# The squared tiles of a scan group summed on VectorE before the matmul with ones, and the sum moved one product on

## The chip, the cores and the metric

The kernel runs on one core of a Trainium2 chip. The metric is the device time of one execution in microseconds. TensorE does the matrix products into PSUM (eight banks of 128 partitions by 512 floats), VectorE and ScalarE do elementwise work, GpSimd a little of it, and SyncE starts the transfers. Each engine has its own program, in order; they are held together by semaphores.

## The reference

A trunk of two layers over 256 latent tokens and 256 context tokens of width 1024. Layer 0 has a mixer of Fourier channel groups and a bidirectional state-space scan (SSD) in four head groups of 384 channels; layer 1 has attention; each is followed by a squared-ReLU MLP. The change sits in the output of the scan:

```python
def ssd_output(y, xs, z, d_skip, norm_g):
    b, l = y.shape[:2]
    y = (y + d_skip[..., None] * xs).reshape(b, l, SSD_INNER) * jax.nn.silu(z.astype(jnp.float32))
    yg = y.reshape(b, l, SSD_GROUPS, SSD_INNER // SSD_GROUPS)
    yg = yg * lax.rsqrt(jnp.mean(yg * yg, axis=-1, keepdims=True) + NORM_EPS)
    return (yg.reshape(b, l, SSD_INNER) * norm_g.astype(jnp.float32)).astype(z.dtype)
```

So for every token and head group the squares of 384 channels are averaged, and the group is scaled by one over the root. In the kernel the channels lie on partitions: a group is XT = 3 tiles of 128 channels by 512 tokens, and a sum over channels is a sum over partitions and over the three tiles.

## The kernel before

`script()` writes one list of steps, and every engine walks the same list and does its own part of each step. The order of the list is thus the order on every engine.

Every big product (`gemm`) is a weight tile of 1024 by 128 against 512 tokens. It is split into three products of rounded floats (`a_hi`, `a_lo`, `w_hi`, `w_lo`), 24 matmuls of 128x512 (L1936). At a `gemm` step ScalarE makes the high half of the weight that is used two products later (L1049), and VectorE its low half (L1419). For a `conv` product ScalarE copies the result out of PSUM (L1220, L1223); one product later VectorE adds the four other taps of the convolution (step `taps`, L1629).

The layer-0 scan goes over G = 4 head groups. In group g the list has, in this order:

- `slot(0)`: a product (for group g+1, or z tiles);
- `states`, six scan states. TensorE multiplies into three PSUM banks in turn (L2160); VectorE takes each bank into `hent` (L1688, L1690, L1693). A state can only start when VectorE has emptied the bank of the state three before it;
- between the third and the fourth state, `ysum` of group g-1: TensorE multiplies the three tiles of squares in `gate` by a matrix of ones (L2212), and ScalarE turns the result into the inverse root, Ln and Exp (L1287, L1289);
- `seg`: ScalarE makes a decay tile (L1275, L1278), VectorE multiplies it (L1705);
- `slot(1)`, then `xskip` on ScalarE (L1262);
- `ynorm` of group g-1: VectorE scales the three tiles of that group (L1746);
- four chunks n = 0 to 3, each with `yoff` (TensorE L2187, VectorE L1716), a `seg` or two, `slot(2 + n)`, and `y` (TensorE L2200 and L2204), one chunk later `yt` (VectorE L1732);
- two more products, then `ygate`: VectorE multiplies the group by its gate (L1739), ScalarE squares the three tiles into `gate` (L1282).

Behind the last group the list has `gemm outA 3`, `ysum` of group 3, `gemm outA 4`, four splits, `gemm outA 5`, `ynorm` of group 3. A `gemm` of the kind `outA` ends on VectorE with the residual (L1438). The adding of a gate tile (L1428) for the next z product waits for the `ysum` of the group before.

The TensorE part of the step is:

```python
                elif k == "ysum":
                    pe.wait_ge(ysq_done, st[1] + 1)
                    ...
                    for i in range(XT):
                        ins = mm(ps[:, b, :], ones, gate[:, i, :], start=(i == 0), stop=(i == XT - 1))
                    ins.then_inc(filling(st), 1)
```

Of the kernel before, what the change touches and what calls it, by code (L numbers as in the profile page):

```python
# [14 lines left out]
ALU = mybir.AluOpType  # L15
# [20 lines left out]
G = 4  # L36
# [3 lines left out]
XT = GX // P  # L40
# [121 lines left out]
def script():  # L162

    s = [("vecs",)]
# [57 lines left out]
    for g in range(G):  # L222
        zs = [("z", XT * g + i) for i in range(XT)]
        if g < G - 1:
            convs = [("conv", t) for t in conv_tiles(g + 1)]
            slots = convs + [None] * (5 - len(convs)) + zs
        else:
            slots = zs + [None] + [("outA", m) for m in range(4)]

        def slot(n):  # L230
            if slots[n]:
                gemm(*slots[n])

        def states(i, n):
            for d, ch in STATES[i:i + n]:
                s.append(("state", g, d, ch))

        def mixsplits(half, *tiles):
            if g == G - 1:
                s.extend(("mixsplit", half, f) for f in tiles)  # L240
        ch = SCAN_F
        if g == 0:
            for c_ in ch:
                s.append(("toks", g, c_))
                fill(1)
            unit_done()
            s.append(("cb", g))
            s.append(("seg", g, "f", ch[0]))
        slot(0)
        states(0, 3)  # L250
        if g:
            s.append(("ysum", g - 1))
        states(3, 3)
        s.append(("seg", g, "b", ch[0]))
        mixsplits(0, 0)
        last = g == G - 1
        if last:
            s.extend(("xskip", g, i) for i in range(XT))
            s.append(("seg", g, "f", ch[1]))
        slot(1)  # L260
        if not last:
            s.extend(("xskip", g, i) for i in range(XT))
        if g:
            s.append(("ynorm", g - 1))
        mixsplits(0, 1)
        for n in range(NCH):
            if n:
                s.append(("yt", g, ch[n - 1]))
            s.append(("yoff", g, ch[n]))
            if n < NCH - 1 and not last:  # L270
                s.append(("seg", g, "f", ch[n + 1]))
            mixsplits(0, *((), (2, 3), (6, 7), ())[n])
            if last and n == 0:
                s.append(("seg", g, "b", ch[1]))
            slot(2 + n)
            if last and 0 < n < NCH - 1:
                s.append(("seg", g, "f", ch[n + 1]))
            mixsplits(0, *((), (4,), (), ())[n])
            if n < NCH - 1 and not (last and n == 0):
                s.append(("seg", g, "b", ch[n + 1]))  # L280
            mixsplits(0, *((), (5,), (), ())[n])
            s.append(("y", g, ch[n]))
        s.append(("yt", g, ch[-1]))
        slot(6)
        if g < G - 1:
            s += [("toks", g + 1, c_) for c_ in ch[:2]]
            s.append(("cb", g + 1))
            slot(7)
            s += [("toks", g + 1, c_) for c_ in ch[2:]]
            s.append(("seg", g + 1, "f", ch[0]))  # L290
        s.append(("ygate", g))
# [32 lines left out]
    n = len(ATTN)  # L324
# [37 lines left out]
def trunk(nc, x, ctx, w_mod, vectors, w_ff1, w_ff2, w_in_even, w_dt, w_out_even, w_in_odd, rpb_na, w_out_odd,  # L362
# [45 lines left out]
    for st in steps:  # L408
        k = st[0]
# [124 lines left out]
    with ExitStack() as stack:  # L534
# [69 lines left out]
        gate = place("gate", [P, XT, T])  # L604
# [52 lines left out]
        ident, tle, tge, ones = (c0[:, P * i:P * i + P] for i in range(4))  # L657
# [8 lines left out]
        for name, w in (("cos", SEQ), ("sin", SEQ), ("perm", P), ("dup0", P), ("dup1", P), ("heads", P),  # L666
# [18 lines left out]
        ps = stack.enter_context(nc.psum_tensor("ps", [P, 8, 512], F32))  # L685
# [7 lines left out]
        rows_in = [[sem(f"rows_in{i}{d}") for d in "fb"] for i in range(3)]  # L693


        names = ("arow_done rows_out coef_half grow_done htok_done unit_done sines_done hv_done mfull_done dtrow_done acc_sq tmp_sq mu_used row_done mcol_done modc_done sil_done hi_done lo_done c0_in dft_in xsq_done xrms_done xr_done xn_done xnt_done xu_done c1_in vec_in wdt_in bias_in dve_seq act_seq consts_set vt_done "
                 "silc_done th0_done h_done sq_done var_done rstd_done nt_done u_done split_done coef_done "
                 "wdthi_done wdtlo_done dtv_done dte_done dtln_done dt_done dtx_done uf_done vf_done pad_done acc_done "
                 "th_done xbc_done hs_done btok_done xdt_done xw_done ent_done seg_done g_done y_done zt_done gate_done gated "
# [1 line left out]
                 "vT_done vtok_done kd_done max_done exp_done rs_done prob_done pT_done pv_done ohi_done "  # L701
                 "tap_done xskip_done fin_done out_in vhi_done vsplit_done pair_used zr_done cvec_done crow_done ccol_done shift_done shh_done shl_done uo_done ahi_done").split()
        S = {n: sem(n) for n in names}
        (arow_done, rows_out, coef_half, grow_done, htok_done, unit_done, sines_done, hv_done, mfull_done, dtrow_done, acc_sq, tmp_sq, mu_used, row_done, mcol_done, modc_done, sil_done, hi_done, lo_done, c0_in, dft_in, xsq_done, xrms_done, xr_done, xn_done, xnt_done, xu_done, c1_in, vec_in, wdt_in, bias_in, dve_seq, act_seq,
         consts_set, vt_done, silc_done, th0_done, h_done, sq_done, var_done, rstd_done, nt_done,
         u_done, split_done, coef_done, wdthi_done, wdtlo_done, dtv_done, dte_done, dtln_done, dt_done, dtx_done,
         uf_done, vf_done, pad_done, acc_done, th_done, xbc_done, hs_done, btok_done, xdt_done, xw_done, ent_done, seg_done,
# [65 lines left out]
        qk_n = {q[1:]: i for q, i in count("gemm", ("qn", "kn", "qw", "kw")).items()}  # L773
        hn_n, rot_n = count("hnorm"), count("rot")
        hi_on_act = {q: i for i, q in enumerate([q for q in steps if q[0] == "mixsplit" and (q[1] == 1 or q[2] < 2)])}
        cb_n, hstats = count("cb"), steps_of("hstat")
        dirs = {"f": 0, "b": 1}
        scans = {"f": SCAN_F, "b": SCAN_B}
# [633 lines left out]
        def _(dve):  # L1412
            v = nc.vector
            signal, freeing, latest, counts = ledger()
# [49 lines left out]
            for st in steps:  # L1464
                k = st[0]
# [18 lines left out]
                elif k == "mcol":  # L1484
                    j = st[1]
                    b = jobs[st][0]
# [17 lines left out]
                elif k == "xnt":  # L1504
                    b = jobs[st][0]
# [8 lines left out]
                elif st == NORM0 or k == "half":  # L1514
# [3 lines left out]
                    ins = v.scalar_tensor_tensor(out=coefA[:, f0:f0 + HT, :], in0=mod[:, 0, KT + f0:KT + f0 + HT, :], scalar=1.0,  # L1518
                                                 in1=gmixT[:, 0, f0:f0 + HT].unsqueeze(2).broadcast_to([P, HT, 2]), op0=ALU.add, op1=ALU.mult)
# [59 lines left out]
                elif k == "dtraw":  # L1579
                    b = jobs[st][0]  # L1580
                    dve.wait_ge(*filled(st))
                    v.tensor_copy(dtrow[:, :], ps[0:2 * NH, b, :]).then_inc(signal(dtrow_done), 1)
                elif k == "dtcol":
                    b = jobs[st][0]
# [18 lines left out]
                elif k == "gemm":  # L1603
                    if st not in ready_units:
                        low(unit[st] + AHEAD)
                    b, _ = jobs[st]
# [11 lines left out]
                elif k == "taps":  # L1618

                    t = st[1]  # L1620
                    n = conv_n[("gemm", "conv", t)]
# [9 lines left out]
                elif k == "silu":  # L1631
                    t = st[1]
                    n = conv_n[("gemm", "conv", t)]
                    g = [t in conv_tiles(g) for g in range(G)].index(True)
# [9 lines left out]
                elif k == "dftw":  # L1644
                    if st[1]:
                        dve.wait_ge(*filled(("dfts", st[1] - 1)))
                    for q in range(2):
                        b = jobs[st + (q,)][0]
                        dve.wait_ge(*filled(st + (q,)))
                        v.tensor_copy(vf[:, 2 * q:2 * q + 2, :], ps[:, b, :].rearrange("p (c f) -> p c f", c=2)).then_inc(signal(vf_done), 1)  # L1650
                elif k == "dfts":
                    b = jobs[st][0]
# [8 lines left out]
                elif k == "toks":  # L1661

                    _, g, ch = st
# [6 lines left out]
                    b = jobs[st][0]  # L1670
# [5 lines left out]
                elif k == "state":  # L1676
                    _, g, d, ch = st
                    di = dirs[d]
                    old, new = entering(d, ch), scans[d].index(ch)
                    b = jobs[st][0]  # L1680
# [13 lines left out]
                elif k == "cb":  # L1694
                    b = jobs[st][0]
# [10 lines left out]
                elif k == "yoff":  # L1706
                    _, g, ch = st
                    n = yo_n[st]
# [15 lines left out]
                elif k == "yt":  # L1724
# [5 lines left out]
                    dve.wait_ge(xskip_done, XT * (g + 1))  # L1730
                    part = mixF[:, FN_T + XT * g:FN_T + XT * g + XT, P * ch:P * ch + P]
                    v.tensor_tensor(part, part, ps[:, b, 0:GX].rearrange("p (i l) -> p i l", i=XT), ALU.add).then_inc(freeing(key), 1)  # L1732
                elif k == "ysum" and st[1] == G - 2:
                    gating(("gemm", "z", XT * (G - 1)))
                elif k == "ygate":
# [191 lines left out]
        def _(pe):  # L1927
# [42 lines left out]
            for st in steps:  # L1970
                k = st[0]
# [234 lines left out]
                elif k == "ysum":  # L2206
                    pe.wait_ge(ysq_done, st[1] + 1)
                    b = jobs[st][0]
                    if free_before[st]:
                        pe.wait_ge(*emptied(st))  # L2210
                    for i in range(XT):
                        ins = mm(ps[:, b, :], ones, gate[:, i, :], start=(i == 0), stop=(i == XT - 1))  # L2212
                    ins.then_inc(filling(st), 1)
                elif k == "grow":
                    pe.wait_ge(modc_done, NR0 + MG1)
# [269 lines left out]
```

## Time and profile before

| | |
|---|---|
| time, median of 3 runs | 1194.53 us (1194.1 to 1195.05) |
| the profiled execution's own time | 1193.66 us |
| its span, first to last instruction | 1191.9 us |
| TensorE busy | 1159.9 us (97%) |
| VectorE busy | 840.6 us (71%) |
| ScalarE busy | 616.9 us (52%) |
| scan groups, as seen by the sums of L2212 | 203.1 to 393.3 us |
| mean granted TensorE clock | 0.998 |

Busy shares are of the span. A row of a timeline gives start, duration, engine, line, operation, tiles and count; the bracket at its end is the idle time ahead of it and what ended it. Durations of matmuls overlap, so the pace of a stream is read from the starts.

### The profile page before, as it was taken

How to read it: one execution, taken by the hardware profiler on the slowest of the kernel's cores; microseconds unless marked ns; L12 is line 12 of the kernel's file. 1: busy time of each engine (PE TensorE's matmuls, PEld its weight loads, DVE VectorE, ACT ScalarE, POOL GpSimd, SP SyncE). 2: the span in 40 equal slices, each digit the busy share in tenths (PEclk: the TensorE clock that was granted, in tenths of full speed). 3: DMA queues.
4: the chain of work that ended last, by engine and by line, in shares of the span. 5: the costliest groups of instructions: out<-in, count | busy, mean ns of one | idle time of the engine just before them, and what ended most of it. 6: DMA issues, size and time to landing. Idle time of an engine off the chain costs nothing.

```text
span 1191.9 us, 17207 instructions
## 1 busy us (share of the span) xinstructions
PE 1159.9 (97%) x6430; PEld 930.6 (78%) x6430; DVE 840.6 (71%) x1208; ACT 616.9 (52%) x1074; POOL 84.4 (7%) x73
## 2 busy tenths in 40 slices
PE   5999999999999999999999999999999999999998
PEld 3677677787867787887887887887887579998997
DVE  4563687988978666893882882897777977654655
ACT  5541485949584547622422422446855777654552
POOL 0000101010100042000000000043000004000000
PEclk9999999999999999999999999999999999999999
DMA  9855543342422233644634634631343005555554
GB/s 362 345 182 216 191 143 100 106 125 80 124 80 82 90 125 117 219 146 142 232 123 142 229 119 144 229 122 66 126 136 128 2 4 175 162 192 177 194 182 154
DMA packets 49893, 179.13 MB, mean 150 GB/s; under 512 B 5216, under 2 KB 7584, under 8 KB 47776
## 3 DMA queue, kind: packets, MB, share of 16 engines
q1 hardware_dynamic: 49536, 177.66, 43.5%
q8 instruction: 43, 0.70, 0.2%
q10 hardware_dynamic: 288, 0.56, 0.1%
q14 instruction: 26, 0.21, 0.1%
HBM read 177.05 MB, written 1.15 MB: 150 GB/s over the span
## 4 chain that ended last, share of the span: by engine, by line
PE 84%; DVE 8%; DMA 3%; ACT 3%; issue 2%; SPq 0%; DVEq 0%; ACTq 0%
PE ps L1936 54%; PE ps L1943 9%; PE ps L2230 7%; PE ps L2028 2%; PE ps L2200 2%; DVE sm L1884 2%; DMA mhalf<-in_w_mod 1%; PE ps L1959 1%; PE ps L2187 1%; PE ps L2204 1%; PE ps L2141 1%; DVE ps L1882 1%; DVE prob L1909 1%; DMA xload<-in_ctx 1%; ACT w_hi L1049 1%
## 5 line engine op out<-in xcount | busy, mean ns | idle before, releaser
L1419 DVE TENSOR_TENSOR w_lo<-raw,w_hi 128x1024 fp32r<-128x1024 f32 x206 | 262.6, 1275 | 91.2 <-ACT w_hi L1049 91.2
L1049 ACT ACTIVATE w_hi<-raw 128x1024 fp32r<-128x1024 f32 x206 | 216.8, 1053 | 192.2 <-DMA raw<-in_w_ff 155.6
L1936 PE MATMUL ps<-a_hi,w_hi 128*128 128x512 f32 (+1 forms) x820 | 299.1, 365 | 0.0
L1936 PE MATMUL ps<-a_hi,w_lo 128*128 128x512 f32 (+1 forms) x820 | 288.9, 352 | 0.0
L1936 PE MATMUL ps<-a_lo,w_hi 128*128 128x512 f32 (+1 forms) x820 | 288.7, 352 | 0.0
L1936 PEld LDWEIGHTS ps<-a_hi,w_hi 128*128 128x128 f32 x820 | 155.1, 189 | 26.0 <-issue 2.7
L1936 PEld LDWEIGHTS ps<-a_lo,w_hi 128*128 128x128 f32 x820 | 155.2, 189 | 23.1 <-issue 1.0
L1936 PEld LDWEIGHTS ps<-a_hi,w_lo 128*128 128x128 f32 x820 | 155.0, 189 | 21.3
L1936 PE MATMUL ps<-b_hi,w_hi 128*128 128x512 f32 x304 | 119.2, 392 | 0.0
L1936 PE MATMUL ps<-b_lo,w_hi 128*128 128x512 f32 x304 | 118.5, 390 | 0.0
L1936 PE MATMUL ps<-b_hi,w_lo 128*128 128x512 f32 x304 | 118.3, 389 | 0.0
L1797 DVE SCALAR_TENSOR_TENSOR macc<-mring,silc,macc 128x1536 f32<-128x1536 f32 x56 | 103.5, 1889 | 0.0
L1369 ACT ACTIVATE hr<-ps 128x512 f32<-128x512 f32 x30 | 17.9, 596 | 98.4 <-PE ps L1936 65.7
L1943 PE MATMUL ps<-a_hi,w_hi 128*128 128x512 f32 (+1 forms) x188 | 67.0, 356 | 1.5 <-DVE a_lo L1758 0.4
L1936 PEld LDWEIGHTS ps<-b_hi,w_hi 128*128 128x128 f32 x304 | 57.1, 188 | 14.4 <-DVE hT L1823 1.9
L1936 PEld LDWEIGHTS ps<-b_hi,w_lo 128*128 128x128 f32 x304 | 57.1, 188 | 11.9
L1936 PEld LDWEIGHTS ps<-b_lo,w_hi 128*128 128x128 f32 x304 | 57.1, 188 | 11.6
L1943 PE MATMUL ps<-a_lo,w_hi 128*128 128x512 f32 (+1 forms) x188 | 64.9, 345 | 0.0
L1943 PE MATMUL ps<-a_hi,w_lo 128*128 128x512 f32 (+1 forms) x188 | 64.9, 345 | 0.0
L1629 DVE SCALAR_TENSOR_TENSOR cacc<-cpad,vec,cacc 128x512 f32<-128x512 f32 x80 | 60.1, 752 | 5.9 <-ACT cacc L1223 0.7
L1275 ACT ACTIVATE ey<-ey,acum 128x128 f32<-128x128 f32 x192 | 59.3, 389 | 0.0
L1823 DVE SCALAR_TENSOR_TENSOR hT<-ps,mod,hT 128x256 f32<-128x256 f32 x64 | 27.9, 477 | 43.0 <-PE ps L1936 43.0
(289 smaller groups left out, 1762.3 us busy)
## 6 DMA issues: line engine op xcount, KB each, us to landing
raw<-in_w_ff SPq DMA_DIRECT2D x128, 512.0 KB, 3.5
mring<-in_w_mod SPq DMA_DIRECT2D x32, 768.0 KB, 5.3
raw<-in_w_in_even SPq DMA_DIRECT2D x36, 512.0 KB, 5.8
mring<-in_w_mod SPq DMA_DIRECT2D x16, 1024.0 KB, 5.1
ey<-acum_rows SPq DMA_DIRECT2D x32, 384.0 KB, 5.0
raw<-in_w_in_odd SPq DMA_DIRECT2D x18, 512.0 KB, 3.5
mhalf<-in_w_mod SPq DMA_DIRECT2D x16, 512.0 KB, 9.6
raw<-in_w_out_even SPq DMA_DIRECT2D x16, 512.0 KB, 3.5
```

Source lines behind the costliest of these rows:

```text
L1049: nc.scalar.activation(w_hi[:, u % RING, :, :], raw[:, u % RING, :, :], ACT.Copy).then_inc(hi_done, 1)
L1275: nc.scalar.activation(ey[:, di, r, :], ey[:, di, r, :], ACT.Relu, scale=-1.0, bias=acum[:, st[3], head_col(st) + r:head_col(st) + r + 1]) ...
L1419: v.tensor_tensor(w_lo[:, u % RING, :, :], raw[:, u % RING, :, :], w_hi[:, u % RING, :, :].bitcast(F32), ALU.subtract).then_inc(lo_done, 1)
L1629: v.scalar_tensor_tensor(out=acc, in0=cpad[:, n % 2, :, w:w + SEQ], scalar=convwT[:, w, t:t + 1], in1=acc, op0=ALU.mult, op1=ALU.add).then ...
L1797: ins = v.scalar_tensor_tensor(out=macc[i][:, :], in0=row, scalar=weight, in1=macc[i][:, :], op0=ALU.mult, op1=ALU.add)
L1823: ins = v.scalar_tensor_tensor(out=hs, in0=ps[:, b, SEQ * i:SEQ * i + SEQ], scalar=mod[:, L, 5 * KT + m, i:i + 1], in1=hs, op0=ALU.mult, o ...
L1884: v.tensor_reduce(sm[:, 3, i % 3, :], ps[:, b:b + 2, :], AX, ALU.max).then_inc(signal(dve_seq), 1)
L1936: ins = mm(out_ap, w_[:, n % RING, k, :], (x_[k][:, 0:ntok] if type(x_) is list else x_[:, k, 0:ntok]), start=(k == 0 and j == 0), stop=(k ...
L1943: ins = mm(outs[i], w_[:, tiles_[i] % RING, k, :], (x_[k][:, 0:ntok] if type(x_) is list else x_[:, k, 0:ntok]), start=(k == 0 and j == 0) ...
L2028: ins = mm(ps[:, LEAD_BANKS[i], 0:ntok], w_[:, slot + i, kk, :], x_[:, kk, c_:c_ + ntok], start=(kk == 0 and q == 0), stop=(kk == KT - 1 a ...
L2200: mm(ps[HD * par:HD * par + HD, b, P * i:P * i + P], xdt[:, di, ch, HD * r:HD * r + HD], ey[:, di, r, :], start=(i == 0 and di == 0), stop ...
L2230: ins = mm(ps[:, B_TOK[q], :], x_[:, m, P * t:P * t + P], moving_rows(w_, u, half), start=(begin and j == 0), stop=(end and j == 2))
```

## The change

In groups 0, 1 and 3 VectorE adds the three tiles of squares in place, tile 1 to tile 0 and then tile 2, and TensorE multiplies one tile by ones in place of three. Group 2 keeps its three matmuls. In the list, the `ysum` of groups 0 and 1 (which stand in groups 1 and 2) moves from between the states to where `ynorm` stood, behind `slot(1)` and `xskip`; their `ynorm` moves behind `slot(2)`. The `ysum` of groups 2 and 3 and their `ynorm` stay where they were. The new semaphore `group_sq` tells TensorE that the adds are done. The diff without the lists of semaphore names:

```diff
         slot(0)
         states(0, 3)
-        if g:
+        if g == G - 1:
             s.append(("ysum", g - 1))
         states(3, 3)
...
         slot(1)
         if not last:
             s.extend(("xskip", g, i) for i in range(XT))
-        if g:
+        if g == G - 1:
             s.append(("ynorm", g - 1))
+        elif g:
+            s.append(("ysum", g - 1))
         mixsplits(0, 1)
...
             slot(2 + n)
+            if n == 0 and 0 < g < G - 1:
+                s.append(("ynorm", g - 1))
...
+        summed = {g: i + 1 for i, g in enumerate(g for g in range(G) if g != G - 2)}
...
+                elif k == "ysum" and st[1] in summed:
+                    dve.wait_ge(ysq_done, st[1] + 1)
+                    v.tensor_tensor(gate[:, 0, :], gate[:, 0, :], gate[:, 1, :], ALU.add).then_inc(signal(dve_seq), 1)
+                    dve.wait_ge(*latest())
+                    v.tensor_tensor(gate[:, 0, :], gate[:, 0, :], gate[:, 2, :], ALU.add).then_inc(signal(group_sq), 1)
...
-                    for i in range(XT):
-                        ins = mm(ps[:, b, :], ones, gate[:, i, :], start=(i == 0), stop=(i == XT - 1))
+                    parts = 1 if st[1] in summed else XT
+                    if st[1] in summed:
+                        pe.wait_ge(group_sq, summed[st[1]])
+                    for i in range(parts):
+                        ins = mm(ps[:, b, :], ones, gate[:, i, :], start=(i == 0), stop=(i == parts - 1))
                     ins.then_inc(filling(st), 1)
```

## Rows read from the trace of the kernel before

**Rows 1.** The page: span, busy time, and busy tenths in 40 slices.

```profile
PE 1159.9 (97%) x6430; PEld 930.6 (78%) x6430; DVE 840.6 (71%) x1208; ACT 616.9 (52%) x1074; POOL 84.4 (7%) x73
...
DVE  4563687988978666893882882897777977654655
```

**Rows 2.** Windows of group 1: stretch, us, busy time by engine, clock, DMA.

```profile
200.00:215.00 15.00, 14.63 (x52) 9.22 (x51) 11.25 (x16) 11.84 (x18) 1.62 (x2) 1.00 0.11 35
215.00:255.00 40.00, 40.00 (x254) 32.01 (x254) 37.05 (x51) 30.06 (x64) 0.00 (x0) 1.00 0.49 144
```

**Rows 3.** Timeline of TensorE in group 1.

```profile
203.07 2.84 PE L2212 MATMUL ps<-gate,c 128*128 128x512 f32 x6
205.83 0.88 PE L2160 MATMUL ps<-xw,btok 128*128 128x384 f32 x2
...
207.74 0.88 PE L2160 MATMUL ps<-ycomb,btok 128*128 128x384 f32 x2 [0.37 <-DVE hent L1693]
...
213.93 0.81 PE L2187 MATMUL ps<-hent,xbc 128*128 128x384 f32 x2
...
228.60 1.53 PE L2200 MATMUL ps<-ey,xdt 128*64 128x128 f32 x24
```

**Rows 4.** Timeline of VectorE in group 1.

```profile
203.99 1.23 DVE L1419 TENSOR_TENSOR w_lo<-raw,w_hi 128x1024 fp32r<-128x1024 f32 x1 [2.50 <-ACT w_hi L1049]
205.13 1.21 DVE L1688 COPY hent<-ps 128x384 f32<-128x384 f32 x2
206.45 0.56 DVE L1690 TENSOR_TENSOR hent<-hent,dt_tot 128x384 f32<-128x384 f32 x1
207.04 0.55 DVE L1693 TENSOR_TENSOR hent<-hent,ps 128x384 f32<-128x384 f32 x1
...
210.79 0.56 DVE L1693 TENSOR_TENSOR hent<-hent,ps 128x384 f32<-128x384 f32 x1
211.73 0.96 DVE L1705 TENSOR_TENSOR ey<-ey,cbm 128x768 f32<-128x768 f32 x1 [0.38 <-ACT ey L1278]
212.83 3.11 DVE L1629 SCALAR_TENSOR_TENSOR cacc<-cpad,vec,cacc 128x512 f32<-128x512 f32 x4
215.86 1.22 DVE L1419 TENSOR_TENSOR w_lo<-raw,w_hi 128x1024 fp32r<-128x1024 f32 x1
217.00 2.07 DVE L1746 SCALAR_TENSOR_TENSOR mixF<-mixF,vec,gate 128x512 f32<-128x512 f32 x3
...
226.05 0.95 DVE L1705 TENSOR_TENSOR ey<-ey,cbm 128x768 f32<-128x768 f32 x1
```

**Rows 5.** TensorE instructions of line 2212: durations in ns, minimum, median, maximum.

```profile
L2212 PE MATMUL ps<-gate,c x24: 590/592/697, 203.1 to 393.3; 128*128 128x512 f32 x24
```

**Rows 6.** VectorE instructions of line 1758, the same columns.

```profile
L1758 DVE TENSOR_TENSOR b_lo<-mixF,b_hi x8: 691/692/695, 400.4 to 417.5; 128x512 fp32r<-128x512 f32 x8
```

**Rows 7.** Timeline of ScalarE in group 1.

```profile
204.34 0.77 ACT L1223 ACTIVATE cacc<-ps,vec 128x512 f32<-128x512 f32 x1
...
208.96 1.85 ACT L1275 ACTIVATE ey<-ey,acum 128x128 f32<-128x128 f32 x6
...
217.19 1.86 ACT L1275 ACTIVATE ey<-ey,acum 128x128 f32<-128x128 f32 x6
```

**Rows 8.** Timelines of TensorE and VectorE in group 2.

```profile
280.99 0.81 PE L2187 MATMUL ps<-hent,xbc 128*128 128x384 f32 x2
...
284.03 2.07 DVE L1746 SCALAR_TENSOR_TENSOR mixF<-mixF,vec,gate 128x512 f32<-128x512 f32 x3
```

**Rows 9.** Timelines of TensorE and VectorE around the sum of group 3.

```profile
391.11 2.73 PE L2212 MATMUL ps<-gate,c 128*128 128x512 f32 x6
...
392.25 0.87 DVE L1438 SCALAR_TENSOR_TENSOR hT<-ps,mod,hT 128x256 f32<-128x256 f32 x2
```

**Rows 10.** Timeline of TensorE at the start of the kernel.

```profile
25.79 0.64 PE L1959 MATMUL ps<-mhalf,sil 128*32 128x256 f32 x8 [1.89 <-DMA mhalf<-in_w_mod]
27.14 0.81 PE L1959 MATMUL ps<-mhalf,sil 128*32 128x256 f32 x8 [0.71 <-DMA mhalf<-in_w_mod]
```

**Rows 11.** Windows; after the five busy times, granted clock, DMA share, GB/s.

```profile
27.00:31.00 4.00, 3.85 (x27) 1.58 (x27) 3.93 (x7) 1.94 (x4) 0.00 (x0) 0.57 1.05 387
920.00:924.00 4.00, 1.13 (x9) 0.72 (x8) 2.60 (x5) 3.19 (x7) 0.00 (x0) 1.00 0.40 131
```

More of the change, by code:

```diff
@@ L693, in trunk @@
         rows_in = [[sem(f"rows_in{i}{d}") for d in "fb"] for i in range(3)]
-        names = ("arow_done rows_out coef_half grow_done htok_done unit_done sines_done hv_done mfull_done dtrow_done acc_sq tmp_sq mu_used row_done mcol_done modc_done sil_done hi_done lo_done c0_in dft_in xsq_done xrms_done xr_done xn_done xnt_done xu_done c1_in vec_in wdt_in bias_in dve_seq act_seq consts_set vt_done "
+        names = ("group_sq arow_done rows_out coef_half grow_done htok_done unit_done sines_done hv_done mfull_done dtrow_done acc_sq tmp_sq mu_used row_done mcol_done modc_done sil_done hi_done lo_done c0_in dft_in xsq_done xrms_done xr_done xn_done xnt_done xu_done c1_in vec_in wdt_in bias_in dve_seq act_seq consts_set vt_done "
                  "silc_done th0_done h_done sq_done var_done rstd_done nt_done u_done split_done coef_done "
@@ L703, in trunk @@
         S = {n: sem(n) for n in names}
-        (arow_done, rows_out, coef_half, grow_done, htok_done, unit_done, sines_done, hv_done, mfull_done, dtrow_done, acc_sq, tmp_sq, mu_used, row_done, mcol_done, modc_done, sil_done, hi_done, lo_done, c0_in, dft_in, xsq_done, xrms_done, xr_done, xn_done, xnt_done, xu_done, c1_in, vec_in, wdt_in, bias_in, dve_seq, act_seq,
+        (group_sq, arow_done, rows_out, coef_half, grow_done, htok_done, unit_done, sines_done, hv_done, mfull_done, dtrow_done, acc_sq, tmp_sq, mu_used, row_done, mcol_done, modc_done, sil_done, hi_done, lo_done, c0_in, dft_in, xsq_done, xrms_done, xr_done, xn_done, xnt_done, xu_done, c1_in, vec_in, wdt_in, bias_in, dve_seq, act_seq,
          consts_set, vt_done, silc_done, th0_done, h_done, sq_done, var_done, rstd_done, nt_done,
```

## The prediction

> **What bounds the kernel now.** I read the page first. TensorE is busy for 97% of the span and VectorE for 71%, and in slices 7 to 13, the scan groups, VectorE stands at 8 to 9 tenths [rows 1]. So the average says "TensorE-bound", and work taken from TensorE ought to shorten the run. The windows make it finer: from 200 to 215 us VectorE is busy for 11.25 us of 15, from 215 to 255 us for 37.05 us of 40, while TensorE is busy throughout [rows 2]. Both engines run close together. So the question is which of them arrives first where they meet, and for that I read the timelines of one scan group engine by engine (group 1, from 203 us).
>
> TensorE finishes its states, does the three matmuls of the sum of group 0 in the middle of them (203.07 us), waits 0.37 us for VectorE's third scan product, does the sixth state at 207.74, then the second conv product, and starts the off-diagonal product (L2187) at 213.93 [rows 3]. VectorE is behind it: entering states until 211.35, seg at 211.73, four conv taps at 212.83, the low half of a weight at 215.86, and only at 217.00 what stands next in its order, the norm of group 0 [rows 4]. It had no gap of its own from 203.99 on but the 0.38 us ahead of seg. TensorE does not notice, because nothing that it needs in these microseconds comes from that work.
>
> **The change, part by part.**
>
> *What TensorE is spared.* One 128x512 matmul with ones is two records [rows 5]; the six of a group run from 203.07 to 205.83, so three cost 2.76 us and one costs 0.92. Two matmuls less are 1.84 us a group. Groups 0, 1 and 3 change, so 5.5 us of TensorE work go; group 2 keeps its three matmuls and its place.
>
> *Taking the sum out from between the states of groups 1 and 2.* This buys nothing. State 6 writes the bank of state 3 and waits until VectorE has emptied it. That is done at 207.59 (207.04 plus 0.55) [rows 4], and it hangs on the low half at 203.99 and the copies at 205.13, none of which depend on the sum. With the sum gone TensorE waits there instead, and state 6 still starts at 207.74, the conv product still ends at 213.93. The 2.76 us had filled a wait.
>
> *The adds.* The trace has no 128x512 add of two SBUF tiles in these places, but the same operation class and shape stands in L1758: 692 ns [rows 6]. The second add waits for the first; a dependent one in the scan chain starts 0.03 us after the end of the one before (206.45 plus 0.56, to 207.04) [rows 4]. So 0.69 + 0.03 + 0.69 = 1.41 us. A bound from below is two of 384 columns, 2 x 0.55 = 1.1 us, from above two of 768 columns, 2 x 0.96 = 1.9 us [rows 4]; I take 1.41, since L1758 has the very shape.
>
> *Where they stand.* In VectorE's order the adds come where the norm stood, at 217.00. ScalarE's Ln, Exp and two table loads no longer stand ahead of its first backward decay tile, which began at 208.96, although ScalarE was through with the conv's copy at 205.11 [rows 7]. That removes VectorE's 0.38 us wait before 211.73, so the adds start at about 216.65 and end at 218.06. TensorE reacts some 0.15 us later (207.59 to 207.74 is the same reaction): 218.2. It has been ready since 213.93. So TensorE waits 4.3 us, then sums for 0.92, and L2187 starts at 219.1 in place of 213.93: **+5.2 us**. Everything after L2187 on TensorE follows without a wait until the group's end, and VectorE's own waits near the group's end hang on TensorE's gate products, so the delay is passed on whole. Queued behind the waiting matmul are L2187, the third product and all that follows; ScalarE's Ln waits too, with the decay tiles behind it.
>
> *Group 2.* The same rows stand 67 us later: L2187 at 280.99, the norm on VectorE at 284.03, which is 3.04 us behind (3.07 in group 1) [rows 8]. **+5.2 us** again.
>
> *Group 3's own sum.* Before, TensorE begins it at 391.11, straight behind the product outA 3. Now the adds stand behind VectorE's residual of outA 3, which itself waits for that product and ends at 393.12 [rows 9]. Adds until 394.55, matmul at 394.7: 3.6 us later, less the 1.84 us of two matmuls, **+1.8 us**. TensorE idles some 3.3 us of it, once the last product has drained.
>
> *The moved second half.* ynorm goes one product later in groups 1 and 2. Its 2.07 us on VectorE are moved, not added; it is due before the next gating of that tile, tens of microseconds later. No DMA, no SyncE or GpSimd instruction is in the moved steps. The order of banks does not change.
>
> Waits and matmuls together: 5.2 + 5.2 + 1.8 = 12.2 us.
>
> *The clock.* At the start of this trace TensorE idled 1.89 us and a little later 0.71 us, and its granted clock then fell to the lower level, 1.2 GHz [rows 10]; the window from 27 to 31 us has a mean of 0.57, so 3.4 us of it ran at half and 1.7 us were lost [rows 11]. But between 920 and 924 us, with 1.13 us busy of 4, it stayed at 1.00 [rows 11]. The two new waits of 4.3 us are longer than all of these idle times, the third (3.3 us) hardly. For each the loss is bounded by 0 and 1.7 us, 0 to 5.1 us over the three; it is under 1.7 where part of the slow stretch lies in the wait itself. I take one fall behind each of the two 4.3 us waits at 1.5 us, none behind the third: +3.0. The Trainium skill, "TensorE: Matmul & The Clock Gate", section "What's actually happening", says that throttled is the default state and that activity releases the clock. By that rule taken strictly all three waits would be followed by a slow stretch, and the sum would be 2.1 us higher; rows 10 agree with it, the stretch at 920 us does not.
>
> Sum: 12.2 + 3.0 = 15.2 us. The profiled execution took 1193.66 us (span 1191.9 and 1.76 around it), which makes 1208.9; it lies 0.87 us under the median of 1194.53, and against that the forecast is **1209.7 us**.
>
> **The rivals.**
> - *Waits without a fall of the clock.* For it: rows 11. Against: 4.3 us in one piece is more than that stretch had in all. 1194.5 + 12.2 = 1206.7.
> - *A second lag behind it.* ScalarE now does Ln and Exp at about 219.3 to 222.0, ahead of the forward decay tile that it did from 217.19 [rows 7]. That tile comes at 224.6, VectorE's taps and low half follow it, and the next backward seg, at 226.05 before [rows 4], ends near 233.5. TensorE wants it at 228.60 + 5.2 = 233.8 [rows 3]. By this count it holds by 0.3 us; if it fails, TensorE waits 1 to 2 us more in each of two groups: with the falls, 1209.7 + 3 = 1213.
> - *The adds come in time (the other side).* If VectorE had them done by 213.93, TensorE would save all 1.84 x 3 = 5.5 us: 1189.0. It decides at one point: the adds must start by 212.5, and in order VectorE stands at the taps then [rows 4]. It would need to be 4 us earlier on a chain that has 0.38 us of waiting in it; or it would have to take the adds ahead of their turn, once the squares are there, and every row of its timeline is in program order. The Trainium skill, "TensorE: Matmul & The Clock Gate", section "Architectural detail", calls VectorE's queue strict first-in first-out, which by itself excludes the second way; the trace agrees (212.83, 215.86, 217.00, as the script has them).
> - *The delay is absorbed.* VectorE is busy for 37.05 of 40 us in the stretch behind L2187 [rows 2]; if it, and not TensorE, paced that stretch, only its added 1.4 us a group would count, some 2.8 us, and with the 1.8 us of group 3 the time would be 1199.1. Against: TensorE is busy for all 40 us of that stretch, so a delay ahead of it finds nothing to go into.
> - *The change does nothing on the path*: 1194.5, against all of the above.
>
> **How the numbers follow.** Forecast 0.45; no fall 0.25; second lag 0.12; absorbed 0.10; in time 0.05; nothing 0.03. Changes under about 0.2% (2.4 us) can't be told here from none. Faster 0.05, same 0.03, slower 0.92. The range takes in the first three cases and the bounds of the adds and the clock (0 to 5.1 us): below, 12.2 less 0.3 for each pair of adds and about 1.3 for a VectorE that gets there somewhat sooner is 10.0, or 1204.5; above, all three falls of the clock and half of the second lag, 1194.5 + 12.2 + 5.1 + 2 = 1214 (rounded up).
>
> **What would show it.** In the new profile: TensorE's records of L2212 fall from 24 to 12; ahead of them, by VectorE's add, about 4.2 us of idle time twice and 3.3 once; states 4 and 5 with short waits for VectorE; state 6 no earlier than before; L2187 5.2 us later in group 1; the next seg close to TensorE's need; PEclk below 1.00 right behind the long waits. The forecast is wrong if VectorE does the adds before TensorE is through with the second conv product, or if the clock stays at 1.00 (then 3 us too high), or if the slow stretch lasts much longer than 3.4 us (too low).

## The result and the profile after

The changed kernel takes 1212.49 us (median of 4 runs, 1211.97 to 1213.29), against 1194.79 us before in the same comparison: ratio 1.0149, 95% interval 1.0136 to 1.0161. It is 17.7 us slower. The profiled execution took 1211.97 us with a span of 1210.2 us, 18.3 more than before. It lies inside the recorded range (1204.5 to 1214.0), 2.8 us above the point.

The page of the changed kernel, the lines that answer to [rows 1]. The mean granted clock is 0.994, and was 0.998 before.

```profile
span 1210.2 us, 17189 instructions
PE 1161.3 (96%) x6418; PEld 930.6 (77%) x6418; DVE 845.1 (70%) x1214; ACT 616.6 (51%) x1074; POOL 84.5 (7%) x73
...
DVE  4563687786979466985684784797778976755555
```

The busy times hardly move: VectorE has six adds more and 4.5 us more busy time; TensorE has 12 records fewer and yet 1.4 us more busy time. So the loss is in waits, and in matmuls that run slower. Who TensorE waited for, 190 to 425 us of the changed kernel (us in total, times, longest):

```profile
PE ps L2225 <- DVE gate L1742: 10.6, 3, 4.2
PE ps L2170 <- DVE hent L1693: 5.3, 2, 2.7
PE ps L2214 <- DVEq L1728: 1.7, 2, 0.9
```

L2225 is the sum, L1742 the second add, L2170 the states. The third line is no news: the kernel before waits the same 1.7 us at that instruction. Group 1 of the changed kernel, VectorE first (this answers to [rows 4]; the lines lie five further on, and the adds are L1740 and L1742):

```profile
211.44 0.96 DVE L1710 TENSOR_TENSOR ey<-ey,cbm 128x768 f32<-128x768 f32 x1
212.54 3.12 DVE L1634 SCALAR_TENSOR_TENSOR cacc<-cpad,vec,cacc 128x512 f32<-128x512 f32 x4
215.58 1.22 DVE L1424 TENSOR_TENSOR w_lo<-raw,w_hi 128x1024 fp32r<-128x1024 f32 x1
216.71 0.69 DVE L1740 TENSOR_TENSOR gate<-gate 128x512 f32<-128x512 f32 x1
217.44 0.69 DVE L1742 TENSOR_TENSOR gate<-gate 128x512 f32<-128x512 f32 x1
220.12 0.56 DVE L1721 TENSOR_TENSOR ycomb<-ps,dt_ea 128x384 f32<-128x384 f32 x1 [1.99 <-PE ps L2197]
224.95 0.96 DVE L1710 TENSOR_TENSOR ey<-ey,cbm 128x768 f32<-128x768 f32 x1 [4.27 <-ACT ey L1283]
...
231.03 2.07 DVE L1756 SCALAR_TENSOR_TENSOR mixF<-mixF,vec,gate 128x512 f32<-128x512 f32 x3
233.21 0.96 DVE L1710 TENSOR_TENSOR ey<-ey,cbm 128x768 f32<-128x768 f32 x1
```

and TensorE (it answers to [rows 3]; L2197 was L2187, L2210 was L2200):

```profile
205.82 1.06 PE L2170 MATMUL ps<-xw,btok 128*128 128x384 f32 x2 [2.67 <-DVE hent L1693]
...
218.27 1.10 PE L2225 MATMUL ps<-gate,c 128*128 128x512 f32 x2 [3.13 <-DVE gate L1742]
219.21 0.81 PE L2197 MATMUL ps<-hent,xbc 128*128 128x384 f32 x2
...
234.22 1.53 PE L2210 MATMUL ps<-ey,xdt 128*64 128x128 f32 x24 [0.27 <-DVE ey L1710]
```

The adds end at 218.13 and TensorE starts 0.14 us later; L2197 is 5.28 us later than L2187 was. VectorE's next forward seg waits 4.27 us for ScalarE, and the seg behind it makes TensorE wait for 0.27 us. Groups 2 and 3:

```profile
291.43 1.76 PE L2225 MATMUL ps<-gate,c 128*128 128x512 f32 x2 [4.18 <-DVE gate L1742]
292.98 1.49 PE L2197 MATMUL ps<-hent,xbc 128*128 128x384 f32 x2
...
407.70 1.97 PE L2225 MATMUL ps<-gate,c 128*128 128x512 f32 x2 [3.32 <-DVE gate L1742]
```

One matmul takes 0.94 us from start to start in group 1 and 1.55 in group 2: there the clock had fallen. Windows of the changed kernel (behind the five busy times comes the granted clock):

```profile
206.00:210.00 4.00, 4.00 (x9) 2.21 (x9) 3.58 (x7) 2.64 (x5) 0.00 (x0) 0.57 0.00 0
291.00:295.00 4.00, 3.57 (x6) 1.96 (x7) 0.71 (x2) 2.50 (x3) 0.00 (x0) 0.59 0.00 0
408.00:412.00 4.00, 4.00 (x10) 2.43 (x10) 0.00 (x0) 2.27 (x3) 0.00 (x0) 0.60 0.00 0
939.00:943.00 4.00, 3.09 (x12) 1.64 (x12) 3.50 (x10) 1.51 (x3) 0.00 (x0) 0.66 0.10 39
```

Four stretches at the lower level, 1.2 GHz, each behind a wait. Not every wait brought one: the clock stayed at 1.00 behind the 2.68 us wait at the fourth state of group 2 (window from 277 to 283 us) and behind the 3.13 us wait at the sum of group 1 (from 218 to 224 us). The first one follows the 2.67 us wait at the fourth state and delays the second conv product by 1.0 us, but that only shortens the wait for the adds behind it, from 4.2 to 3.13 us. The last one lies in attention, where the change touches nothing.

Read at the same instruction in both traces, TensorE's delay grows like this:

| place | delay, us | grown by |
|---|---|---|
| group 1, first off-diagonal product | 5.28 | 5.28: wait for the adds, one matmul in place |
| group 2, first state | 6.10 | 0.82: wait for the next seg 0.27, and small waits to the group's end |
| group 2, chunk 0's y | 13.06 | 6.96: 5.28 as in group 1, and 1.68 of slow clock |
| group 3, first state | 13.05 | 0 |
| outB, first product | 16.62 | 3.57: wait 3.54, less 1.84, and 1.87 of slow clock |
| attention, first transposes of V | 16.63 | 0 |
| end of the span | 18.3 | 1.67: the slow stretch at 939 us |

### The profile page after: what moved, and what is told of

It reads as the page before. It is cut to its first block, busy times and chain, and to the rows that moved or that the text cites. A ratio compares the mean times of both kernels' runs of the same rounds, so it can differ in the third digit from the quotient of the medians.

```text
span 1210.2 us, 17189 instructions
## 1 busy us (share of the span) xinstructions
PE 1161.3 (96%) x6418; PEld 930.6 (77%) x6418; DVE 845.1 (70%) x1214; ACT 616.6 (51%) x1074; POOL 84.5 (7%) x73
## 4 chain that ended last, share of the span: by engine, by line
PE 80%; DVE 11%; ACT 4%; DMA 3%; issue 3%; SPq 0%; DVEq 0%; ACTq 0%
PE ps L1946 50%; PE ps L1953 9%; PE ps L2243 7%; PE ps L2038 2%; DVE sm L1894 2%; DMA mhalf<-in_w_mod 1%; PE ps L1969 1%; PE ps L2210 1%; DVE cacc L1634 1%; DVE ey L1710 1%; PE ps L2197 1%; ACT ey L1280 1%; PE ps L2214 1%; PE ps L2151 1%; PE ps L2170 1%
```

## Experiments

Each ratio is against the kernel before as it ran in the same comparison. There it took 1194.51 us beside the runs with one matmul, with only the moves, with group 3 alone and with the waits filled; 1194.85 us beside those with copies, with the adds ahead of the taps, with three matmuls and with the adds early and nothing moved; and 1194.49 us beside the last two.

**The sums of groups 0 and 1 cut to one matmul where they were.** The kernel before; two of three tiles are left out of these sums.

```diff
-                    for i in range(XT):
+                    parts = 1 if st[1] < 2 else XT
+                    for i in range(parts):
```

> The kernel before, its order kept, with the sums of groups 0 and 1 cut to one matmul of the first tile (two of three squared tiles are left out of these sums). Theory: the 2.76 us of matmuls between the states had filled a wait for VectorE's third scan product, so taking 1.84 us out twice buys nothing: L2187 of group 1 stays at 213.9 us, the time within 0.5 us of 1194.8; the fourth state shows a new wait of about 1.8 us. Rival: TensorE's work there is on the path, and the time falls by 3.7 us to 1191.1.

Measured 1194.81 us, ratio 1.0006 (0.9997 to 1.0015). TensorE in group 1:

```profile
203.03 1.12 PE L2213 MATMUL ps<-gate,c 128*128 128x512 f32 x2
205.79 0.88 PE L2160 MATMUL ps<-xw,btok 128*128 128x384 f32 x2 [1.64 <-DVE hent L1688]
...
213.91 0.81 PE L2187 MATMUL ps<-hent,xbc 128*128 128x384 f32 x2
```

The wait takes the place of the matmuls and L2187 stays at 213.9 us. 3.7 us less work on an engine that is busy for 97% of the span bought nothing: in this place TensorE was waiting for VectorE, with matmuls over the wait.

**Only the moves, no adds.** The kernel before with the new places of `ysum` and `ynorm`, three matmuls each.

```diff
-        if g:
+        if g == G - 1:
             s.append(("ysum", g - 1))
...
+        elif g:
+            s.append(("ysum", g - 1))
...
+            if n == 0 and 0 < g < G - 1:
+                s.append(("ynorm", g - 1))
```

> The kernel before with only the two moves (sum of groups 0 and 1 behind the second product, norm one product on), three matmuls, no adds. Theory: the 2.76 us leave a place where they filled a wait and come to stand on the path, so each group costs 2.8 us, 5.5 together, up to 3 more if the clock falls in a wait: 1200 to 1203. Rival: the move is free and all of the loss is the wait for the adds: 1195.

Measured 1205.68 us, ratio 1.0086 (1.0071 to 1.0102): 11.2 us slower, more than the theory had. The sum stands at 214.01 and pushes L2187 by 2.65 us, as expected. But chunk 1's y waits too, in both groups, by 1.97 and 1.96 us. Group 1:

```profile
214.01 2.74 PE L2216 MATMUL ps<-gate,c 128*128 128x512 f32 x6
216.58 0.81 PE L2191 MATMUL ps<-hent,xbc 128*128 128x384 f32 x2
...
233.26 1.53 PE L2204 MATMUL ps<-ey,xdt 128*64 128x128 f32 x24 [1.97 <-DVE ey L1709]
```

This is the recorded rival of the second lag, with no adds in the kernel at all. So in groups 1 and 2 two chains push TensorE back: one over the sum, one over ScalarE (Ln, Exp and their loads, then the decay tile) and VectorE (seg, taps, low half, the moved norm, the next seg). At chunk 1 the second alone gives 4.66 us of delay (233.26 against 228.60 in [rows 3]). ScalarE in that kernel:

```profile
217.38 1.28 ACT L1291 ACT_TABLE_LOAD   x1
218.68 0.69 ACT L1291 ACTIVATE gate<-ps,eps 128x512 f32<-128x512 f32 x1
219.39 1.28 ACT L1293 ACT_TABLE_LOAD   x1
220.68 0.63 ACT L1293 ACTIVATE gate<-gate 128x512 f32<-128x512 f32 x1
221.22 1.85 ACT L1279 ACTIVATE ey<-ey,acum 128x128 f32<-128x128 f32 x6
```

The decay tile starts at 221.22, where it was at 217.19 [rows 7]. The four rows ahead of it are 3.9 us. Before the move they stood directly ahead of the backward decay tile at 208.96 [rows 7], where VectorE lost 0.38 us by them and TensorE nothing. In the kernel before:

```profile
205.13 1.28 ACT L1287 ACT_TABLE_LOAD   x1
...
208.43 0.63 ACT L1289 ACTIVATE gate<-gate 128x512 f32<-128x512 f32 x1
```

The moved norm stands on the same chain, on VectorE directly ahead of the seg that TensorE waits for, here at 230.07 us for 2.07 us; in the changed kernel it is the row at 231.03 above.

**ScalarE's two loads away.** The same kernel; in groups 0 and 1 Ln and Exp are replaced by two copies of the same size, so their norms are no inverse roots.

```diff
-... ps[:, b, :], ACT.Ln, ...
+                    plain = st[1] < 2
+... ps[:, b, :], ACT.Copy if plain else ACT.Ln, ...
-... gate[:, XT - 1, :], ACT.Exp, ...
+... gate[:, XT - 1, :], ACT.Copy if plain else ACT.Exp, ...
```

> The kernel that only moves the sum and the norm, with ScalarE's Ln and Exp of groups 0 and 1 replaced by two copies of the same size, so that the two table loads of 1.28 us fall away (the two norms are then not an inverse root). Theory: the wait of 1.97 us for VectorE's seg, which hung on ScalarE's forward decay tile, goes in both groups: 1205.7 - 3.9 = 1201.8 (1200.5 to 1202.5). Rival: the wait comes from the norm's 2.07 us on VectorE and stays: 1205.7.

Measured 1201.29 us, ratio 1.0053 (1.0037 to 1.0068): 4.4 us less than with the loads. Chunk 1's y has no wait any more:

```profile
232.34 1.53 PE L2205 MATMUL ps<-ey,xdt 128*64 128x128 f32 x24
```

VectorE still does the norm in its new place. So the second chain goes over ScalarE, and shortening it there by the two loads is enough. That the norm is harmless does not follow: its 2.07 us stand on the same chain and are a little more than the wait of 1.97, so by the rows (not by a run; none moved the norm alone) taking it off the chain would have removed the wait as well.

**The adds ahead of the taps.** The changed kernel, with a step of its own for the adds of groups 0 and 1 ahead of the second product.

```diff
         states(3, 3)
         s.append(("seg", g, "b", ch[0]))
+        if 0 < g < G - 1:
+            s.append(("yadd", g - 1))
...
-                elif k == "ysum" and st[1] in summed:
+                elif k == "yadd":
```

> The changed kernel with the two adds of groups 0 and 1 taken ahead of the second product's taps and weight on VectorE, so that they are done when TensorE arrives (213.9 us in group 1). Theory as it stands after the run that only moved the steps: TensorE's wait for the adds goes, but the forward decay tile is still behind Ln, Exp and two table loads on ScalarE, and TensorE waits 3 to 4 us for VectorE's next backward seg instead. Chunk 1's y starts near 233.2 us, 4.6 us later than before, and the time is 1207.5 to 1210. Rival, the recorded prediction's: the wait for the adds is the whole of it, each group then costs 1.1 us: 1194.5 + 2.2 + 4 = 1201.

Measured 1215.4 us (1209.54 to 1216.35), ratio 1.016 (1.0139 to 1.018). The adds are done at 213.77, TensorE sums at 215.04 without a wait (its product was slowed again by the clock, by 1.1 us), and the whole kernel is no faster than the changed one. What it no longer waits for at the sum it waits for at chunk 1:

```profile
213.08 0.69 DVE L1744 TENSOR_TENSOR gate<-gate 128x512 f32<-128x512 f32 x1
...
215.04 1.02 PE L2227 MATMUL ps<-gate,c 128*128 128x512 f32 x2
...
234.28 1.98 PE L2212 MATMUL ps<-ey,xdt 128*64 128x128 f32 x16 [3.64 <-DVE ey L1712]
```

The y of chunk 1 is at 234.28 in this kernel and at 234.22 in the changed one. The rival (1201 us) is out, even by the fastest of the five executions. The excess over the expectation is the clock: behind the 3.64 us wait it stayed low for longer than behind any wait of the changed kernel, as this window shows (0.57 over 8 us is 6.9 us at half). It cost the path 2.7 us: chunk 1's y is 5.68 us later than in the kernel before, chunk 2's 8.39.

```profile
233.00:241.00 8.00, 6.72 (x36) 5.44 (x37) 7.32 (x11) 5.60 (x13) 0.00 (x0) 0.57 0.13 40
```

**Group 3 alone.** The kernel before, with the adds and the single matmul in group 3 only. The line is against the changed kernel, whose moves are undone as well.

```diff
-        summed = {g: i + 1 for i, g in enumerate(g for g in range(G) if g != G - 2)}
+        summed = {G - 1: 1}
```

> The kernel before with the adds and the single matmul in group 3 alone, groups 0 to 2 as before. Theory: TensorE waits about 3.4 us for adds that stand behind the residual of outA 3, saves 1.84, so 1.7 us slower by the wait and up to 1.9 more when the granted clock falls behind it: 1196.5 to 1198.5. Rival (two matmuls less are two matmuls less): 1.8 us faster, 1193.0.

Measured 1199.23 us, ratio 1.0034 (1.0021 to 1.0048): 4.7 us slower, above the expectation. The wait is the expected one, the slow stretch behind it twice as long as I had bounded it:

```profile
394.52 2.05 PE L2221 MATMUL ps<-gate,c 128*128 128x512 f32 x2 [3.32 <-DVE gate L1738]
```

```profile
393.00:400.00 7.00, 5.48 (x11) 3.70 (x12) 1.34 (x3) 3.37 (x4) 0.00 (x0) 0.52 0.12 47
```

0.52 over 7 us is 6.7 us at half. At outB (419.90 against 415.47) the delay is 4.4 us, of which 1.7 are wait and matmuls; so 2.7 us were lost by the clock.

**The waits filled.** The changed kernel with matmuls of constants in TensorE's waits, into the bank that the sum overwrites.

```diff
+                    if 0 < g < G - 1 and n % len(STATES) == 3:
+                        pe.wait_ge(*emptied(("ysum", g - 1)))
+                        for i in range(2):
+                            mm(ps[:, B_TR, :], ones, c0[:, 0:4 * P], start=True, stop=True)
...
                     if st[1] in summed:
+                        for i in range(4 if st[1] < 2 else 3):
+                            mm(ps[:, b, :], ones, c0[:, 0:4 * P], start=True, stop=True)
```

> The changed kernel with matmuls of constants put into TensorE's waits: two ahead of the fourth state in groups 1 and 2, four ahead of the sum there, three ahead of the sum in group 3, all into the bank that the sum then overwrites. Theory: the waits end as before but the granted clock stays at full, which gives back the two slow stretches behind the sums, 1.7 and 1.9 us: 1209 (1208.5 to 1209.8). Rival: the slow stretches don't come from the waits, or cost nothing: 1212.5 or a little more.

Measured 1209.38 us, ratio 1.0123 (1.0108 to 1.0139), 3.1 us under the changed kernel. 15 matmuls whose results are thrown away make it faster. The waits that are left in these places are 0.7 us at the sums and 1.0 us at the fourth states, and the clock does not fall:

```profile
286.00:300.00 14.00, 13.33 (x67) 8.74 (x66) 7.63 (x11) 12.11 (x20) 0.00 (x0) 1.00 0.11 39
```

The two profiled executions can be set side by side at the first transposes of attention, ahead of the slow stretch at 939 us, which this execution did not have. There the delay is 13.48 us (933.28 against 919.80) in place of 16.63: 3.15 us come back of the 3.55 that the clock had cost up to there.

**Three matmuls behind the adds.** The changed kernel; the sum counts two tiles twice.

```diff
-                    parts = 1 if st[1] in summed else XT
+                    parts = XT
```

> The changed kernel, adds and waits as they are, but the sum still takes three matmuls in every group (its value then counts tiles 1 and 2 twice). Theory: TensorE is on the path in all three places, so 1.84 us three times come back: 1212.5 + 5.5 = 1218. Rival: in groups 1 and 2 something else sets the end and only group 3 pays: 1214.3.

Measured 1216.65 us (1214.71 to 1221.03), ratio 1.0176 (1.016 to 1.0191): 4.2 us over the changed kernel, between the two and nearer to the theory. The matmuls saved are on the path here; the 0.3 us wait at chunk 1 is gone in exchange, and the clock adds its own scatter, so that 4.2 against 5.5 can't be split further.

**The adds early, nothing moved.** VectorE adds right behind the squares, in groups 0, 1 and 3; the sums of groups 0 and 1 stay between the states, that of group 3 goes behind outA 4.

```diff
         s.append(("ygate", g))
+        if g != G - 2:
+            s.append(("yadd", g))
...
```

> The kernel before with the adds of groups 0, 1 and 3 on VectorE directly behind the squares (ahead of the next weight's low half, where VectorE waits anyway), one matmul each; the sums of groups 0 and 1 stay between the states, that of group 3 goes one product later. Theory: adds cost 0.5 us a group on VectorE's chain, the matmuls saved there buy nothing, group 3 saves 1.84: 1193.5 (1192.5 to 1195). Rival: adds on a VectorE that is 9 tenths busy cost their full 1.4 us a group: 1195.5 or more.

Measured 1195.82 us, ratio 1.001 (1.0001 to 1.0019), 2.3 us above the point. Two things were missed. The first add took 1.23 us in group 1 and 1.16 in group 2, not 0.69; there GpSimd was at its last state products at that time (0.69 in group 3, where it was not). So the adds cost VectorE's chain 0.9 us, not 0.5. That GpSimd is the reason is read from this overlap alone; no run took it away. GpSimd, then VectorE:

```profile
202.34 1.62 POOL L1040 TENSOR_TENSOR ycomb<-xdt,dt_dte 128x384 f32<-128x384 f32 x2 [7.78 <-PE ps L2168]
```

```profile
203.28 1.23 DVE L1738 TENSOR_TENSOR gate<-gate 128x512 f32<-128x512 f32 x1 [1.55 <-ACT gate L1285]
204.54 0.69 DVE L1740 TENSOR_TENSOR gate<-gate 128x512 f32<-128x512 f32 x1
205.15 1.22 DVE L1422 TENSOR_TENSOR w_lo<-raw,w_hi 128x1024 fp32r<-128x1024 f32 x1
```

And TensorE's gap is now cut in two, 1.98 us ahead of the sum and 0.51 behind it (1.92 and 0.51 in group 2), and the clock fell in both groups:

```profile
205.38 1.10 PE L2223 MATMUL ps<-gate,c 128*128 128x512 f32 x2 [1.98 <-DVE gate L1740]
206.98 1.37 PE L2168 MATMUL ps<-xw,btok 128*128 128x384 f32 x2 [0.51 <-DVE hent L1691]
```

```profile
204.00:212.00 8.00, 6.12 (x14) 3.29 (x15) 7.30 (x13) 7.91 (x15) 0.00 (x0) 0.79 0.03 13
```

By the next product 2.0 us were lost in group 1 and 1.7 in group 2 (L2187's place, less the 0.24 us by which this execution ran later from the start), which is twice group 3's gain of 1.8. But against the changed kernel it is 16.7 us faster: the adds themselves were never dear.

**Group 3 alone, with the adds early.** The kernel before; adds behind the squares and ahead of outA 3, and in one of the two also the sum behind outA 4.

```diff
+    s.append(("yadd", G - 1))
     gemm("outA", 3)
-    s.append(("ysum", G - 1))
     gemm("outA", 4)
+    s.append(("ysum", G - 1))
```

> The same adds directly behind the squares in group 3, but TensorE's matmul stays where it was, behind outA 3. Theory: the adds end near 391.6 us, TensorE wants them at 391.1, waits about 0.6 us and saves 1.84: 1.2 us faster than before, 1193.6, no fall of the clock near 400 us; against the run with group 3 changed as in the change, 1199.2, it is 5.6 us faster, which is the price of the adds' place. Rival: the price is in the adds themselves and stays: 1198 or more.

> The kernel before with a change in group 3 alone: VectorE adds the squares directly behind ScalarE's squaring, ahead of outA 3's weight, and TensorE's single matmul goes one product later, behind outA 4. Groups 0 to 2 as before. Theory: no engine waits for the adds, the 1.84 us of two matmuls are saved on the path: 1192.9 (1192.0 to 1194.0), no fall of the clock near 400 us. Rival: something else behind outA 4 (norm, splits) takes the gain back: 1194.8.

With the sum left behind outA 3: 1194.04 us, ratio 0.9989 (0.998 to 0.9998). With the sum behind outA 4: 1193.4 us, ratio 0.9988 (0.9979 to 0.9997). The first waited 0.46 us for the adds, and neither shows a fall of the clock near 400 us; both times lie within half a microsecond of what was expected. Both intervals end below 1, if only just, and the gain is 0.1%. TensorE and VectorE in the second:

```profile
396.54 1.02 PE L2222 MATMUL ps<-gate,c 128*128 128x512 f32 x2
```

```profile
390.15 0.69 DVE L1737 TENSOR_TENSOR gate<-gate 128x512 f32<-128x512 f32 x1 [1.55 <-ACT gate L1284]
390.88 0.69 DVE L1739 TENSOR_TENSOR gate<-gate 128x512 f32<-128x512 f32 x1
391.49 1.22 DVE L1421 TENSOR_TENSOR w_lo<-raw,w_hi 128x1024 fp32r<-128x1024 f32 x1
```

The adds stand for the most part where VectorE stood still for ScalarE's high half (2.50 us idle ahead of L1419 before); the low half starts 0.38 us later for them (391.49 against 391.11), and no wait of TensorE comes of it. And the transposes of attention start at 918.08 in place of 919.80, 1.72 us earlier. The last kernel is the one to keep; 5.8 us lie between it and group 3's edit as the change makes it, by nothing but the place of two adds and a matmul; 2.7 of them are the slow clock behind the wait that the place made.

## Why the prediction came out right, and where it did not

*The work spared between the states buys nothing.* Right, and shown alone: with one matmul in place of three and nothing else changed, 1.0006.

*The adds in order at 216.65 to 218.06, TensorE at 218.2, L2187 5.2 us later, twice.* Measured 216.71 to 218.13, 218.27, and 5.28 in group 1. In group 2 L2197 is 5.89 us further behind, of which 0.61 is the slow clock in the one matmul (1.55 in place of 0.94), and 5.28 again is left. In group 3 +1.8 was forecast and 1.70 measured. Together 12.2 forecast, 12.26 measured.

*That the wait for the adds is the whole of it in groups 1 and 2.* The sum stands, but this reading of it does not, and the total hides it. The prediction put the moved second half at nothing, and gave the second lag 0.12 as something that might come on top. It did come, by 0.27 us at that place. But it is a second chain of nearly the same length, not an addition: with no adds it alone gives 4.7 us (the run with only the moves), with the adds on time it makes the kernel as slow as it was. The move costs groups 1 and 2 most of their loss (11.2 us with only the moves and three matmuls; the changed kernel's 17.7 less group 3's 4.7 is 13.0); the adds' wait lies beside it. I had the numbers for it ("it holds by 0.3 us") and read them as a margin where they said that two chains end together.

*The clock.* 3.0 us were forecast, for two falls at 1.5; 1.68 and 1.87 were lost. That the total came so near is luck in part, since they were not both where I put them: one fell behind the 4.2 us wait of group 2, the other behind the 3.3 us wait of group 3, and group 1's fell already behind the 2.67 us wait at the states, where it cost nothing, since TensorE had to wait for the adds anyway. The prediction had called the waits at the states short. The filled waits show the cause: 3.1 us come back. The bound of 1.7 us for a fall was too low: slow stretches of 6.7 and 6.9 us were seen, and 2.7 us were lost on the path by each. By the Trainium skill, "TensorE: Matmul & The Clock Gate", section "What's actually happening", activity releases the throttle. The trace agrees in that all four slow stretches of the changed kernel began behind a wait and ended while TensorE was multiplying; behind the waits of 2.68 and 3.13 us named above there was none.

*What was not in the sum.* 0.5 us of small waits to the end of group 1, and 1.67 us at 939 us. That last stretch is not the change's: the kernel before has a wait of 2.42 us in the same place, inside the window at 920 us of [rows 11], and kept its clock, while it fell there in 8 of the 12 profiled executions. Those with group 3 early are among them, and their medians are below the kernel before's all the same.

```profile
922.82 0.63 PE L2392 MATMUL ps<-c,prob 128*128 128x128 f32 x4 [2.42 <-ACT vtok L1267]
```

Executions of the kernel before without a trace had mean granted clocks from 0.995 to 1.000 and took 1193.2 to 1197.3 us, so slow stretches come and go in it too. Why the clock falls in one execution and not in the next with the same wait was not settled.

*In time, absorbed, nothing.* The rival of the adds in time was priced wrongly, at 1189.0 us. It let all three pairs of spared matmuls count, though by the prediction's own second part the two between the states bought nothing, and the one matmul left in each group now stands on the path; and it had no second chain. With the adds in time in groups 1 and 2 the kernel took 1215.4 us, 1209.54 at the fastest. In the changed kernel itself the three rivals are excluded, by the wait of 10.6 us in total and the delays that nothing took back between group 1's chunk 1 and the end.

## What to carry to other kernels

Work may stand over a wait. Before you take it out of a busy engine, ask when the next instruction behind it could start without it; here that was 207.59 us, sum or no sum, and 3.7 us of matmuls were worth nothing.

When a step is moved, walk it on each engine by itself. This one was walked on TensorE and VectorE; its ScalarE part (two activations and two table loads, 3.9 us) moved to where a decay tile is due that VectorE and then TensorE wait for, the norm's 2.07 us moved into the same chain, and together they set the time as much as the adds did. And when two chains end within a few tenths, repairing either one gains next to nothing: test them both.

Two adds of 0.69 us were cheap behind the squares, where their engine was idle, and cost 3.5 us of TensorE's time two steps further on. Place them by when the input is ready and the engine idle, not beside their reader.

## What the runs showed of the hardware

A wait of TensorE can cost more than its length. Behind waits of 2.4 to 4.2 us the granted clock often stood at half, for 3.4 us or for about twice that, with some 1.7 or 2.7 us lost where TensorE set the pace; behind others of the same length (2.42, 2.68, 3.13 us) it did not fall. A gap of 2.5 us cut in two by one matmul was enough in both groups where it was tried. Filling the waits with matmuls whose results are thrown away kept the clock up and made the kernel 3.1 us faster.

An add of 128x512 on VectorE took 0.69 us alone and 1.16 and 1.23 us where GpSimd's products ran beside it.
